# Router logits taken during the conformer's second projection, a new routing order, and square-root tables loaded ahead of their use

## What is computed

```
x = x + conformer_conv(rmsnorm(x, norm_mix_odd))            # ends in  silu(layernorm(c)) @ conf_w2 + conf_b2
h = rmsnorm(x, norm_ffn_odd)                                # x * rsqrt(mean(x*x) + eps) * gain
logits = h @ router                                         # 1024 x 8
top_v, top_i = lax.top_k(logits, 2)
gates = softmax(top_v)
x = x + sum over e of gate_e * ((silu(h @ wg[e]) * (h @ wu[e])) @ wd[e])
y = rmsnorm_final(x)
```

## Time and profile before

| | |
|---|---|
| median of 3 runs | 1540.28 us (1539.86 to 1540.58) |
| the profiled execution's own time | 1540.19 us |
| its span in the trace | 1538.5 us |
| mean granted TensorE clock | 0.963 of full |
| PE busy | 1444.9 us (94%) |
| DVE busy | 372.5 us (24%) |
| ACT busy | 204.4 us (13%) |
| DMA, mean over the span | 240 GB/s |

### The profile page before, as it was taken

The page is one execution under the profiler, slowest core; times in us unless marked ns, Lnnn a source line. Parts: engine busy times, 40 slices in busy tenths (PEclk is TensorE's granted clock), DMA queues, the critical chain, the costliest instruction groups (busy, mean ns, idle before and its releaser), DMA issues.

```text
span 1538.5 us, 18649 instructions
## 1 busy us (share of the span) xinstructions
PE 1444.9 (94%) x7779; PEld 933.9 (61%) x7779; DVE 372.5 (24%) x829; ACT 204.4 (13%) x444; POOL 45.8 (3%) x75
## 2 busy tenths in 40 slices
PE   7999799899999998989799999999999999999887
PEld 6886678778888887867666544434443443434433
DVE  3527825310000004992500010100102002011012
ACT  2232303110000002322300000000000000000001
POOL 2003200000000100000000000000000000000000
PEclk9999979999999999999799999999999999999998
DMA  8534503246446433100299799998999987989995
GB/s 274 191 114 150 179 0 111 92 130 199 132 142 225 131 109 108 57 4 1 85 400 374 246 364 404 397 388 315 399 403 397 384 317 277 383 324 403 399 399 200
DMA packets 230662, 369.56 MB, mean 240 GB/s; under 512 B 8989, under 2 KB 192717, under 8 KB 230524
## 3 DMA queue, kind: packets, MB, share of 16 engines
q1 hardware_dynamic: 226133, 355.54, 63.8%
q0 software_dynamic: 2448, 8.91, 1.9%
q10 hardware_dynamic: 2002, 3.95, 0.9%
HBM read 362.30 MB, written 7.16 MB: 240 GB/s over the span
## 4 chain that ended last, share of the span: by engine, by line
PE 83%; DVE 9%; DMA 3%; SPq 2%; ACT 1%; issue 1%; DVEq 0%; ACTq 0%
PE ps L1538 28%; PE ps L1955 13%; PE ps L2020 11%; PE ps L1970 8%; DVE region L1262 5%; PE ps L1980 4%; PE ps L1884 3%; PE ps L1765 3%; PE ps L2029 2%; PE ps L1547 1%; PE ps L1914 1%; SPq L506 1%; PE ps L1925 1%; PE ps L1615 1%; DMA ring<-in_moe_w_down_dram 1%
## 5 line engine op out<-in xcount | busy, mean ns | idle before, releaser
L1538 PE MATMUL ps<-Ht,ring 128*128 128x264 f32 x1600 | 369.7, 393 | 8.2 <-DVE Ht L1012 6.7
L1538 PEld LDWEIGHTS ps<-Ht,ring 128*128 128x128 f32 x1600 | 308.4, 194 | 69.2 <-issue 12.3
L1955 PE MATMUL ps<-ring,region 128*64 128x352 f32 (+1 forms) x1280 | 232.8, 460 | 8.9 <-DMA ring<-in_moe_w_up_dram 4.3
L1955 PEld LDWEIGHTS ps<-ring,region 128*64 128x64 f32 (+1 forms) x1280 | 121.2, 147 | 117.5 <-issue 80.1
L2020 PE MATMUL ps<-ring,region 128*64 128x512 f32 (+1 forms) x704 | 179.3, 606 | 2.4 <-DMA ring<-in_moe_w_down_dram 1.8
L2020 PEld LDWEIGHTS ps<-ring,region 128*64 128x64 f32 (+1 forms) x704 | 59.5, 146 | 110.2 <-issue 103.4
L1970 PE MATMUL ps<-ring,region 128*64 128x352 f32 x768 | 118.8, 462 | 0.0
L1538 PE MATMUL ps<-region,ring 128*128 128x264 f32 x480 | 110.9, 390 | 3.7 <-ACT region L873 3.7
L1538 PEld LDWEIGHTS ps<-region,ring 128*128 128x128 f32 x480 | 91.9, 192 | 20.4 <-issue 4.1
L1970 PEld LDWEIGHTS ps<-ring,region 128*64 128x64 f32 x768 | 53.2, 137 | 63.2 <-issue 62.8
L1262 DVE SCALAR_TENSOR_TENSOR region<-region,par 128x256 f32<-128x256 f32 x180 | 74.8, 477 | 1.0
(11 more groups left out here) (333 smaller groups left out, 1004.5 us busy)
## 6 DMA issues: line engine op xcount, KB each, us to landing
ring<-in_moe_w_gate_dram SPq DMA_DIRECT2D x128, 704.0 KB
ring<-in_moe_w_up_dram SPq DMA_DIRECT2D x128, 704.0 KB
ring<-in_moe_w_down_dram SPq DMA_DIRECT2D x48, 1536.0 KB
ring<-in_w_in_even_dram SPq DMA_DIRECT2D x10, 2048.0 KB, 9.4
ring<-in_moe_w_down_dram SPq DMA_DIRECT2D x16, 1024.0 KB
ring<-in_ffn_w_gate_dram SPq DMA_DIRECT2D x11, 1024.0 KB, 5.5
ring<-in_ffn_w_up_dram SPq DMA_DIRECT2D x11, 1024.0 KB, 9.1
ring<-in_ffn_w_down_dram SPq DMA_DIRECT2D x4, 2816.0 KB, 10.8
```

The source lines that it names most:

```text
L1538: ins = mm(ps[:, 0:T], w[:, c, cols:cols + P], src[:, c, :], start=c == 0, stop=c == nk - 1)
L1955: ins = mm(out, xg[:, 4 * j + c, 0:cap], w[:, c, r, :], start=j + c == 0, stop=j + c == 4)
```

## The change

There are four parts.

1. The router works on tokens that are not normalised. When DVE has added a chunk of `w2` to `XT`, it at once writes `H = XT * gain` for that chunk. PE multiplies these chunks with the router weights between the projections of `conf2`: chunks 0 to 2 after the fourth tile, then one after each tile, the last one behind the loop. `H` and `htok` are then without the norm's root. The root is brought in per token: a small matmul turns it to token rows (tile `rtok`), DVE takes its reciprocal, and `select` multiplies the selection matrix by it.
2. The order of the routing. PE does three of the six `xt2` tiles, `rtok` and `pos` ahead of the `ht` tiles, and the other three `xt2` tiles last. DVE goes from the mask straight to the order of the experts and `Sel`; the softmax and the table of gates come after the number of rounds. Three comparisons per 64 columns become one per 192 columns, and several pairs of operations are merged.
3. POOL makes the routing constants earlier, before the conformer's second convolution product.
4. ACT runs a one-column Sqrt (`load_root_table`) ahead of the squares in seven places, so that the table of the square root is loaded there.

```diff
-    for i in range(6):
+    for i in range(3):
         add(("xt2", i), ("acc_ready", i + 1))
-    add("lg", ("lg_ready", 2))
+        if i == 0:
+            add("lg", ("lg_ready", 2))
+    add("rtok", ("rtok_ready", 2))
+    add("pos", ("pos_ready", 2))
     for i in range(6):
         add(("ht", i), ("htok_ready", i + 1))
-    add("pos", ("pos_ready", 1))
+    for i in range(3, 6):
+        add(("xt2", i), ("acc_ready", i + 1))
...
+            def load_root_table():
+
+                a.activation(par[:, 508:509], eps[:, 0:1], ACT.Sqrt)
+
...
+            act.wait_ge(sem("eps_ready"), 2)
+            load_root_table()
             for c in range(DC):
                 square(0, c, SQ0)
...
+            load_root_table()
             for c in range(DC):
                 act.wait_ge(sem("gv_cent"), c + 1)
...
+            load_root_table()
             for c in range(DC):
                 act.wait_ge(sem("gated"), c + 1)
...
+            load_root_table()
             for c in range(DC):
                 square(2, c, SQ2)
...
+            load_root_table()
             for c in range(DC):
                 act.wait_ge(sem("cc_cent"), c + 1)
...
+            load_root_table()
             for c in range(DC):
                 square(3, c, SQ2)
             root("norm3", 0)
...
+                    if gain:
+                        dve.wait_ge(sem("res_ready"), 8 * k + c + 1)
+                        v.tensor_scalar(H[:, c, :], XT[:, c, :], col(gain, c), None, ALU.mult).then_inc(
+                            sem("h_ready"), 1)
...
-            residual(2, "w2", "conf_b2")
-            norm(3, "norm_ffn_odd")
...
+            residual(2, "w2", "conf_b2", "norm_ffn_odd")
...
+            then(v.tensor_tensor(c2, lj, le, ALU.is_equal))
+            after(v.tensor_tensor(c1, lj, le, ALU.is_gt))
...
+            v.reciprocal(rtok[:, 0:2], tile("rtok")[:, 0:2]).then_inc(sem("rtok_ready"), 1)
...
-                    ins = v.tensor_scalar(Sel[:, b, 0:cap], iota[:, 0:cap], ptab[:, b, at], None, ALU.is_equal)
+                    ins = v.tensor_scalar(Sel[:, b, 0:cap], iota[:, 0:cap], ptab[:, b, at], rtok[:, b:b + 1],
+                                          ALU.is_equal, ALU.mult)
...
+            def logits(c):
+
+                if c == 0:
+                    for sname, value in TILES[NUM["lg"] - RING][1]:
+                        pe.wait_ge(sem(sname), value)
+                    pe.wait_ge(sem("router_loaded"), 16)
+                    pe.wait_ge(sem("lg_zero"), 1)
+                    mm(lg[:, 0:24], ident[:, :], L, start=True, stop=False)
+                pe.wait_ge(sem("h_ready"), 3 * DC + c + 1)
+                for k in (0, 1, 2) if c < DC - 1 else (1, 2, 0):
+                    n = ROWS[k]
+                    ins = mm(lg[0:n, 8 * k:8 * k + 8], H[:, c, P * k:P * k + n], wr[:, c, :], start=False,
+                             stop=k == 0 and c == DC - 1)
+                return ins
+
...
+                    for c in range(3) if 4 * s + j == 3 else range(4 * s + j - 1, 4 * s + j) if 4 * s + j > 3 else ():
+                        logits(c)
...
+            residual_rows(0)
+            stat("norm3", "sq_ready", 24, SQ2, DC - 1)
+            ins = logits(DC - 1)
+            assert claim("lg") is lg
+            done(ins)
+            residual_rows(1)
+            residual_rows(2)
+            pe.wait_ge(sem("stat_read"), len(STATS))
+            ps = claim("rtok")
```

More of the change, by code:

```diff
@@ L36 @@
 QALL = 4 * QCH
+XT2 = (0, 2, 4, 1, 3, 5)
 DBLK = ((0, 2), (2, 5), (5, 8), (8, 11))
@@ L890, in _ @@
                              ACT.Copy).then_inc(sem("htok_ready"), 1)
+            for m in range(3, 6):
+                residual_rows(m)
             act.wait_ge(sem("gate_diff"), 1)
@@ L1224, in _, with residual @@
                     ins.then_inc(sem("yn_ready"), 1)
-            def residual(k, name, bias=None):
+            def residual(k, name, bias=None, gain=None):
                 for c in range(DC):
@@ L1375, in _ @@
             pk = pt1.rearrange("p (k e j) -> p k e j", k=BLK, e=EXP)
-            for k in range(BLK):
-                after(v.tensor_tensor(pk[:, k], ej(perm), k8a(posm[:, 8 * k:8 * k + 8]), ALU.mult))
-            reach()
+            pe4 = bc(ej(perm), 1, [P, BLK, EXP, EXP])
+            dve.wait_ge(sem("pos_ready"), 1)
+            then(v.tensor_tensor(pk, pe4, bc(k8(posm), 2, [P, BLK, EXP, EXP]), ALU.mult))
+            after(v.memset(rt[:, 700:829], -1000.0))
             then(v.tensor_reduce(pm, pt1.rearrange("p (m j) -> p m j", j=EXP), AX.X, ALU.add))
@@ L1388, in _ @@
             select(SEQ_CAP[0], slice(0, 1))
-            for k in range(BLK):
-                after(v.tensor_tensor(pk[:, k], ej(perm), k8a(gate[:, 8 * k:8 * k + 8]), ALU.mult))
-            reach()
-            then(v.tensor_reduce(gm, pt1.rearrange("p (m j) -> p m j", j=EXP), AX.X, ALU.add))
-            for r in range(XROUNDS + 1):
-                after(v.tensor_copy(gtab[:, :, EXP * r:EXP * (r + 1)], k8(gm)))
-            for r in range(XROUNDS):
-                after(v.scalar_tensor_tensor(out=ptab[:, :, EXP * (r + 1):EXP * (r + 2)], in0=k8(pm),
-                                             scalar=-1000.0 - float(SEQ_CAP[EXP - 1] * r), in1=bc(capv, 1, [P, BLK, EXP]), op0=ALU.add,
-                                             op1=ALU.subtract))
+            v.tensor_copy(cnt, tile("pos")[:, 24:32]).then_inc(sem("pos_ready"), 1)
@@ L1410, in _ @@
             v.tensor_scalar(tint[0:1, 1:2], nrf[0:1, 5:6], 1.0, None, ALU.add).then_inc(sem("rounds_ready"), 1)
+            dve.wait_ge(sem("gate_exp"), 1)
+            then(v.tensor_scalar(gt12[:, 3:6], gt12[:, 0:3], 1.0, None, ALU.add))
+            then(v.reciprocal(gt12[:, 6:9], gt12[:, 3:6]))
+            then(v.tensor_tensor(gt12[:, 9:12], gt12[:, 0:3], gt12[:, 6:9], ALU.mult))
+            then(v.tensor_tensor(k8(m1), k8(m1), bc(gt12[:, 6:9], 2, [P, BLK, EXP]), ALU.mult))
+            then(v.tensor_tensor(k8(m2), k8(m2), bc(gt12[:, 9:12], 2, [P, BLK, EXP]), ALU.mult))
+            then(v.tensor_tensor(gate, m1, m2, ALU.add))
+            then(v.tensor_tensor(pk, pe4, bc(k8(gate), 2, [P, BLK, EXP, EXP]), ALU.mult))
+            then(v.tensor_reduce(gm, pt1.rearrange("p (m j) -> p m j", j=EXP), AX.X, ALU.add))
+            for r in range(XROUNDS + 1):
+                after(v.tensor_copy(gtab[:, :, EXP * r:EXP * (r + 1)], k8(gm)))
+            for r in range(XROUNDS):
+                after(v.scalar_tensor_tensor(out=ptab[:, :, EXP * (r + 1):EXP * (r + 2)], in0=k8(pm),
+                                             scalar=-1000.0 - float(SEQ_CAP[EXP - 1] * r), in1=bc(capv, 1, [P, BLK, EXP]), op0=ALU.add,
+                                             op1=ALU.subtract))
             reach()
@@ L1830, in _ @@
                 stat("lnc_var", "csq_ready", 0, SQ2, c)
+            wr = wrt[:, :].rearrange("p (c n) -> p c n", c=DC)
+            lg = tile("lg")
+            def logits(c):
[11 more added lines that the diff above has]
+                return ins
             for s in range(2):
@@ L1871, in _ @@
             done(ins)
+            for k in range(6):
+                ps = claim(("ht", k))
+                n = ROWS[k // 2]
+                for j in range(4):
+                    c = 4 * (k % 2) + j
+                    ins = tr(ps[0:n, P * j:P * (j + 1)], H[:, c, P * (k // 2):P * (k // 2) + n], ident[:, :])
+                done(ins)
+            for m in range(3, 6):
+                residual_rows(m)
             assert turn[0] == len(TILES)
```

137 lines of the change are left out of this document (60 added, 77 removed).

## The result

The changed kernel takes 1525.89 us (median of 4 runs, 1524.49 to 1528.12), the kernel before, beside it on the same chip, 1540.07 us (4 runs, 1538.55 to 1540.58). The ratio is 0.9911, 95% interval 0.9894 to 0.9928. The profiled execution took 1524.49 us, its span is 1522.6 us (before 1538.5), the mean granted clock 0.974 (0.963).

What follows compares the result with a forecast made beforehand. The serial routing stage was taken to hold back both PE's and the DMA's expert streams. Terms -11.6 + 1.6 + 1.2 + 1.5 - 0.5 = -7.8 us against 1540.19 gave 1532.4 us, range 1528.5 to 1537.0.

Steps and rivals of the forecast that it cites:

- The step that failed: Expert phase: followed back to PE, it moves with its first matmul if the weights move at least as much.
- First expert matmul: Start of the expert phase: 11.6 us earlier by the routing, 7.8 us earlier with the table-load and clock terms.
- Logits: Router matmuls placed between the projections of `conf2`: they lengthen it by 3.7 us, identity matmul included.
- From the end of `conf2`: Routing behind the last projection: about 9 us to the order, 14.6 to the gather, 21 to the first expert matmul.
- Gather: Gather ahead of the experts: starts at 752.4 after the clock falls and rises, then takes 5.7 us at full clock.
- The rival with the low clock through the gather: Routing: clock stays low through transposes and gather, first expert matmul only 8.0 us earlier, 1536.0 us; chance 15%.
- the one with the high clock throughout: Routing: clock stays high, gather starts at 750.6, first expert matmul 13.5 us earlier, 1530.5 us; chance 12%.
- Layer-norm loads: Early table loads: +1.5 to 1.6 us at the gated MLP, +1.5 at the conformer, -0.5 at its input norm.
- the clock term of the gated MLP: Gated MLP's mixing: work shifted 1.6 us later runs at low clock, +1.2 us, possibly from nothing to 3.
- A load that stalls ACT once more: Both layer norms: a table switch stalls ACT by the load's length again, +1.3 us each, 1535.0 us; chance 5%.
- Expert phase by weights: Expert phase follows the weights, not PE: -12.8 us counts in place of -11.6, 1531.2 us; chance 8%.
- Slower by a low clock in `conf2`: Logits between projections pull the clock down: up to +10 us on old work, +2.3 on logits, 1544.7 us; chance 5%.

Runs made afterwards that it cites:

- x3: The kernel before with only the seven early table loads added: 1543.31 us, ratio 1.0021 (1.0007 to 1.0036).
- x12: The changed kernel run again with a comment as the only edit, for a third profile: 1524.03 us in one execution.
- x4: The changed kernel without the early table loads at the two layer norms: 1525.08 us, ratio to before 0.9899.
- x8: The changed kernel without any of the seven early table loads: 1531.09 us, ratio 0.9933.
- x5: The kernel before with two unread 128-column PE matmuls ahead of each block of a 64-column expert scatter: 1535.24 us, ratio 0.9959.
- x6: x4 with two unread 128-column PE matmuls ahead of each block of a 64-column expert scatter: 1523.15 us, ratio 0.9889.
- x1: The kernel before with two DVE memsets, 1.9 us of delay, between the copy of the logits and the comparisons: 1536.5 us in one execution.
- x14: The kernel before with three DVE memsets, 2.85 us of delay, between logits and comparisons: 1542.87 us in one execution.
- x15: The kernel before with four DVE memsets, 3.8 us of delay, between logits and comparisons: 1537.32 us in one execution.
- x9: The kernel before run again with a comment as the only edit, for a second profile: 1538.95 us in one execution.
- x10: The kernel before run again with a comment as the only edit, for a third profile: 1542.04 us in one execution.

## Why the prediction was wrong

**The step that failed** is in the first part: "A phase that is followed back to PE moves with its first matmul". I looked for what could lengthen the phase (weights that come late) and took its 767.9 us as fixed. It became 7.2 us shorter (760.7). The 767.9 held three scatters that had lost their clock, 2.8, 3.3 and, at the end, 1.0 us. The windows of the earlier trace rows stop at 761; one over the experts would have shown 0.86 and 0.87. The sum needed a term of -6 to -7 with a chance, and a range down to about 1525. That it would be this kernel's lot could not be computed from the trace of before: half a microsecond decides.

**First expert matmul: right.** Forecast 7.8 us earlier, measured 8.67. Of the three profiles that each kernel has, these two are the median ones (before 770.21, 770.62, 772.46; after 761.58, 761.95, 764.70).

- *Logits.* Forecast +3.7 us on `conf2`; it grew from 33.13 to 37.34, +4.2. Between the last tiles, 0.47 us for six records is the 0.08 each of the earlier trace rows.
- *From the end of `conf2`:* order after 9.0 us (forecast 8.9), gather after 13.8 (14.6), first expert matmul after 20.3 (21.2).
- *Gather.* 5.60 us at clock 1.00 (forecast 5.7). The clock fell at 749.5, during the transposes, and rose at 752.9, so they took 4.35 us. The rival with the low clock through the gather did not come, and neither did the one with the high clock throughout. The Trainium skill, page TensorE: Matmul & The Clock Gate, PE-mode transpose, says that transposes do not count as work for the clock in the way that matmuls do. Here it rose behind 3.4 us of nothing but transposes, so the trace does not agree.
- *Layer-norm loads.* Forecast +1.6, +1.2 by the clock, +1.5, and -0.5 at the input norm: 3.8 by the start of `conf2`. Measured 3.3, in x3 2.9. The parts were less well sized than the sum, which came near partly by luck. The sums of the gated MLP start 1.1 later, their clock falls too (5.50 us for 16 records, before 3.81), and the matmuls behind the mixing (tile `prevT`) start 5.3 later. Then 2.9 come back by 589.9: 0.5 by the early load at the input norm, as forecast, the rest where the clock is low for shorter stretches than before. At the conformer's layer norm the squares start another 1.4 later, and its sums take 5.25 us and not 5.71: +0.9 in place of +1.5. In the repeat x12 `prevT` starts 2.7 later. So the clock term of the gated MLP is between 1.7 (2.7 less the 1.0 by which its sums start late) and 4.2 (5.3 - 1.1), where 1.2 was forecast, and uneven from execution to execution.
- *A load that stalls ACT once more: no.* The activation behind the load starts 0.02 us after it (172.74 + 1.28, then 174.04). The Trainium skill, page ScalarE: Activation LUTs, What ACT_TABLE_LOAD costs, gives a further drain; no row here shows it.
- *Expert phase by weights: no.* x4 and x8 have the same early order and a long phase.
- *Slower by a low clock in `conf2`: no.* It was 0.95 over 34 us of it, and 0.95 over the same part of it before (700 to 734).

**Shown and not shown.** That the scatters' clock makes 6 us is shown by the traces of x5 and x6 (matmuls alone), by x1, x14 and x15 (delay alone) and by the repeats, and by the times of x5. The times of x6 against x4 do not show it. That the distance to the last rise decides is an ordering of 16 profiles with one delay series, not a run that sets the distance alone. Why the sides change where they do, and why an execution that starts 3 us off comes back to the same distance, stays open. The Trainium skill, page TensorE: Matmul & The Clock Gate, Part 1: The HAM clock gate, calls the chip's watching free-running: it does not start with the kernel. A dependence on place would fit that. But the first fall of the clock stood at 23.0, 22.6 and 21.4 us in the three profiles of before, and the distance at 229.69, 229.68 and 229.71.

## What to carry to other kernels

Ahead of a forecast for a phase that only moves, read the granted clock over that whole phase: a light stretch in it that lost its clock is a term of either sign, here 3 us each. Where PE waits in short gaps inside dense work, a few matmuls without use in those gaps took that chance away here, for 1.3 us (a phase of 761.93 in place of 760.65). A table load is worth moving only to a place where its engine is idle; ahead of squares that a matmul waits for, the load and its one-column Sqrt (1.5 us) cost 1.1 and 1.4 us here, and changed the clock behind them.

## What I had not expected of the hardware

A delay of 1.9 us made the phase 5.4 us shorter (x1), one of 2.85 left it as it was and one of 3.8 made it 7.2 shorter (x14, x15). And executions that differ by 2.3 us in `conf2` agree within 1 us over the 767 us behind the first expert matmul, clock falls included (x9, x10).
